# Two-layer hybrid block on one Trainium2 core: the second block's attention rewritten around pairs of query blocks

## The chip, the cores and the metric

One NeuronCore of a Trainium2 chip runs the whole kernel in one launch. The metric is the device time of one execution in microseconds (us). The engines named below are TensorE (PE; its weight loads are listed as PEld), VectorE (DVE), ScalarE (ACT), GpSimd (POOL) and SyncE (SP), which here issues every DMA.

## What is computed

The program is a first block (a state-space layer, two small attentions and gates) followed by a second block of two layers. The change is inside the second block. There a layer l of the reference does, for 512 latent rows `x` and 256 context rows `xc` of width 2048:

```python
q, k, v, up, uf, g = split_proj(h @ w_in[l])          # 8 query heads, 2 key/value heads of 128
q = apply_axial_rope(rmsnorm_2(q, q_norm_g[l]), cos, sin); k = ...
att = latent_attention(q, k, v, kc, vc)               # softmax over 256 context + 512 latent keys
out = merge_branches(att, up, uf, g, ...)             # concat(att, pool, fourier) * silu(g) @ w_out
x_new = x + gate[:, None] * out
if not last:                                          # layer 0 only
    attc = context_attention(qc, kc, vc)              # context queries, context keys only
    xc = xc + gate_c * merge_branches(attc, upc, ufc, gc, ...)
```

Everything is float32. Large products are made on PE as three products of split operands: each operand is a high part (rounded to the type fp32r) and a low part, the rest, and the sum is hi·hi + hi·lo + lo·hi. Products of plain float32 operands are issued as such, and the trace shows each of them as two matmul records.

## The kernel before

The stages run one after the other, each in a block of its own (`nc.Block()`), with a barrier between blocks. For each of the two layers of the second block: `projections(l)` makes 36 tiles of 128 columns of `h @ w_in` into the DRAM tensor `proj2` (tiles 0 to 7 queries, 8 and 9 keys, 10 and 11 values, 12 to 19 pool and Fourier input, 20 to 27 their gates, 28 to 35 the gates of the eight heads), and beside the tiles does the norms, rotations and the two mixing branches, which go to `mixd`. Then `attention(...)` computes the eight heads, and `out_projection` multiplies by `w_out`.

In `attention` the work is cut into units. A unit is one head and 128 queries. In layer 0 (768 columns: 512 latent, 256 context) a head has six units: four latent ones with 768 keys and two context ones with 256 keys, the context ones first and last. In layer 1 (512 columns) a head has four latent units. Per unit g:

- PE `scores(g)`: plain float32 products of queries and keys (L1417) into one of two PSUM buffers;
- DVE `peak(g)`: maximum over the keys (L1508), times -scale (L1510);
- ACT `exp(g)` with the sum over the keys (L1476, and a short read of the accumulator);
- DVE: reciprocal of the sum (L1525); POOL: a diagonal 128x128 matrix with the reciprocals (L1462);
- PE: six (or two) 128x128 transposes of the probabilities (L1434) into PSUM, and DVE copies them out (L1529) into `pt`.

After the last unit of a head, PE multiplies a matrix of ones by the diagonals (L1442), which gives 1/sum for every query, and makes values times probabilities for the whole head in plain float32 (L1446 for the 512 latent columns, L1449 for the 256 context columns of layer 0). ACT makes the tanh of the gate (L1491), DVE finishes silu (L1535), multiplies by 1/sum (L1539) and by the result (L1548), ACT and DVE split the result into high and low part (L1499, L1514) for the output projection. The head's slice of `mixd` is split too (L1494, L1542). Order on each engine is as written; engines wait for each other's counters. On SP the load of the next head's queries (L1378) stands behind the gate load (L1390), the `mixd` load (L1393) and, in the first head, behind four loads of 1 MB of `w_out` (L409, `prime`).

Of the kernel before, what the change touches and what calls it, by code (L numbers as in the profile page):

```python
# [11 lines left out]
F32 = mybir.dt.float32  # L12
F32R = mybir.dt.float32r
I32 = mybir.dt.int32
ALU = mybir.AluOpType
# [3 lines left out]
P = 128  # L19
# [97 lines left out]
def program(nc, cp, const, rope2, cn_sn, cs, invcnt, pos, x_in, mem_in, ctx_in, w_in, w_mem, w_glu,  # L117
            w_out, w_in2, w_out2, ada_w, ssm_b, ssm_c, pool_w, four_w, out):
    ctx = ExitStack()
    with ctx:  # L120
# [81 lines left out]
        odd_copied, shifted = count("odd_copied"), count("shifted")  # L202
        row_out = [count(f"row_out{i}") for i in range(4)]
# [1131 lines left out]
        def attention(heads, group, units, nkeys, qcols, q_src, k_src, v_src, g_src, chunk0, then, mixed=False):  # L1335
# [11 lines left out]

            th, res, g_sb = take(W if mixed else qcols)[:, 0:qcols], take(W if mixed else qcols)[:, 0:qcols], take(qcols)
            if mixed:
                q_sb, k_sb, v_t = ([xw[:, q * W:q * W + n]] for q, n in ((13, qcols), (14, nkeys), (15, nkeys)))  # L1350
                v_t = v_t[0]
            else:
                q_sb, k_sb, v_t = [take(qcols)], [take(nkeys)], take(nkeys)
# [6 lines left out]
            mix_sb = take(qcols) if mixed else None  # L1360
# [7 lines left out]
            with nc.Block() as block:  # L1368
                @block.sync
                def _(sp):  # L1370
                    for i in range(heads):
                        kv = i // group

                        if i > 1:
                            sp.wait_ge(s_ready.h, s_ready.at(nu * (i - 1)))

                        if i or not mixed:
                            sp.dma_start(q_sb[i % 2], q_src(i)).then_inc(loaded[i % 2].h, 16)  # L1378
                        if i % group == 0 and (i or not mixed):
# [5 lines left out]
                        if mixed and i == 1:  # L1385

                            for q in range(2):
                                sp.wait_ge(stored[q].h, stored[q].at(0))
                        sp.wait_ge(m2.h, m2.at(i))
                        sp.dma_start(g_sb, g_src(i)).then_inc(loaded[5].h, 16)  # L1390
                        if mixed:
                            sp.wait_ge(mixd_lo.h, mixd_lo.at(i))
                            sp.dma_start(mix_sb, mixd[i][:, 0:qcols]).then_inc(mixd_in.h, 16)  # L1393
                        if i == 0:
                            prime(sp, then)
# [69 lines left out]
                def _(act):  # L1465
# [15 lines left out]
                    for i in range(heads):  # L1481
                        for u_ in range(nu):
                            g = nu * i + u_
                            if g + 2 < total:
                                exp(g + 2)
                        act.wait_ge(loaded[5].h, loaded[5].at(16 * (i + 1)))
                        act.wait_ge(m5.h, m5.at(i))
                        if mixed and i == 0:
                            for q in range(2):
                                act.wait_ge(stored[q].h, stored[q].at(0))  # L1490
                        act.activation(th, g_sb, ACT.Tanh, scale=0.5).then_inc(m1.h, 1)  # L1491
                        if mixed:
                            act.wait_ge(mixd_in.h, mixd_in.at(16 * (i + 1)))
                            act.activation(h_hi[:, 8 + i, 0:qcols], mix_sb, ACT.Copy).then_inc(mixd_hi.h, 1)  # L1494
                        if (i + 1) % group == 0 and i + 1 < heads:
                            v_out(i // group + 1)

                        act.wait_ge(m5.h, m5.at(i + 1))
                        act.activation(h_hi[:, chunk0 + i, 0:qcols], res, ACT.Copy).then_inc(m6.h, 1)  # L1499

                @block.vector
                def _(dve):
# [16 lines left out]
                    for i in range(heads):  # L1519
# [20 lines left out]
                        if mixed:  # L1540
                            dve.wait_ge(mixd_hi.h, mixd_hi.at(i + 1))
                            dve.tensor_tensor(h_lo[:, 8 + i, 0:qcols], mix_sb, h_hi[:, 8 + i, 0:qcols].bitcast(F32),  # L1542
                                              ALU.subtract).then_inc(mixd_lo.h, 1)
# [19 lines left out]
            if mixed:  # L1563
                mixd_in.base += 16 * heads
                mixd_hi.base += heads
                mixd_lo.base += heads


# [387 lines left out]
        def projections(l):  # L1956
# [58 lines left out]
            p_gate = cnt  # L2015
            p_th = [sums[g % 2] for g in range(4)]
# [17 lines left out]
            with nc.Block() as block:  # L2034
# [127 lines left out]
                def _(act):  # L2162
                    st = Steps(act, va)

                    def read_out(n, par, segs_):
                        act.wait_ge(w_used.h, w_used.at(n + 1))

                        act.wait_ge(stored[par].h, stored[par].at(8 * (n - par)))
                        for a_, (a, b) in zip(accs(par, segs_), segs_):
                            ins = act.activation(stage[par][:, a:b], a_, ACT.Copy)  # L2170
                        ins.then_inc(staged.h, 1)
# [87 lines left out]
                def _(dve):  # L2259
# [36 lines left out]
                    if l:  # L2296
                        dve.wait_ge(rms_ready.h, rms_ready.at(2))
                        dve.reciprocal(inv_c, rms_c).then_inc(st.step(), 1)
                        dve.wait_ge(st.sem, st.now)
                    for iters, n0, segs, kind in parts:  # L2300
                        def body(i):
                            for j in range(4):
# [122 lines left out]
                        turns(st, iters, body, kind, 5 if kind == "qk" else 0)  # L2425
                    dve.wait_ge(st.sem, st.now)
# [175 lines left out]
            for s, v in ((rope_in, 32), (mix_in, 64), (sq_done, 12), (sums_done, 12), (root_done, 11), (qn_done, 11),  # L2602
                         (rot_done, 11), (rot_read, 10), (q_done, 10), (up_in, 64 * len(tok)), (uf_in, 64), (cnt_in, 64),
                         (pgate_in, 64), (fgate_in, 64), (pool_st, 64), (four_st, 64), (chan_done, 4), (odd_copied, 4), (y_copied, 4),
# [53 lines left out]
        for l in range(LAYERS):  # L2658
            last = l == LAYERS - 1
            projections(l)  # L2660
            units = [(b * P, 0, W) for b in range(TB)]
            if not last:

                units[0:0] = [(T, T, CT)]
                units[5:5] = [(T + P, T, CT)]
            width = T if last else W

            def gate(h):
                return row(proj2, h + 28)[:, 0:width]

            def query(h):
                return row(proj2, h)[:, 0:width]
            attention(HEADS2, HEADS2 // KV2, units, W, width, query, lambda kv: proj2[8 + kv], lambda kv: proj2[10 + kv],
                      gate, 0, lambda n: row(w_out2, n + 16 * l), mixed=True)
# [132 lines left out]
```

## Time and profile before

| what | value |
|---|---|
| runs | 3103.9, 3108.8, 3109.0 us (median 3108.8) |
| the profiled execution, its time | 3112.0 us |
| its span | 3110.3 us |
| PE busy | 2862.3 us (92%) |
| DVE, ACT, POOL busy | 51%, 31%, 14% |
| attention of layer 0, first score product to last result | 1839.5 to 2006.4 us |
| attention of layer 1, the same | 2765.5 to 2903.5 us |

A row of a timeline gives start, duration, engine, line, operation, output and inputs, count; in square brackets is how long the engine had been idle and whose end released it. PE's matmuls are pipelined, so the distance between the starts of neighbours is the cost of one, and a row's own duration is a little more. A row that groups instructions gives busy time, mean ns of one, and idle time before.

### The profile page before, as it was taken

The page shows a single profiled execution, that of the slowest core. Times are in us where ns is not written, and L with a number is a line of the kernel's source. Part 1 is how long each engine was busy: PE and PEld are TensorE (multiplying, and loading weights), DVE is VectorE, ACT ScalarE, POOL GpSimd, SP SyncE. Part 2 cuts the span into 40 slices and gives each one's busy share as a digit, 9 for nine tenths or more (in the row PEclk, how much of TensorE's full clock was granted, in tenths as well). Part 3 has the DMA queues.
Part 4 walks back from the last instruction along what each step waited for, and adds up shares of the span by engine and source line. Part 5 has one row for each costly group of instructions (what it writes and reads, how often), then busy time and mean ns, then how long its engine had stood idle before and what let it go on. Part 6 is the DMA issues. An engine that isn't in the chain of part 4 may idle for free. (4 is left out here: it accounts for less than half of the span.)

```text
span 3110.3 us, 35771 instructions
## 1 busy us (share of the span) xinstructions
PE 2862.3 (92%) x13746; PEld 2186.1 (70%) x13746; DVE 1596.3 (51%) x2138; ACT 956.8 (31%) x1601; POOL 450.5 (14%) x609
## 2 busy tenths in 40 slices
PE   7899999988448999999999998899989999989897
PEld 5666666676226867888888875488878877865685
DVE  6678778776554443125533337622243374547434
ACT  4444444443333333122211113311132232223221
POOL 2544444425101021000000001000010000001000
PEclk9999999999669999999999999999999999999998
DMA  5577777762123233233323332222213344431421
GB/s 196 189 303 291 289 299 285 302 241 100 48 88 108 95 126 125 75 115 132 115 100 133 120 136 69 102 76 93 89 77 118 138 163 145 164 135 62 156 95 54
DMA packets 111684, 447.15 MB, mean 144 GB/s; under 512 B 11440, under 2 KB 19760, under 8 KB 76208
## 3 DMA queue, kind: packets, MB, share of 16 engines
q1 hardware_dynamic: 111536, 445.16, 39.1%
q8 instruction: 95, 1.56, 0.2%
q14 instruction: 53, 0.43, 0.0%
HBM read 375.25 MB, written 69.86 MB: 143 GB/s over the span
## 5 line engine op out<-in xcount | busy, mean ns | idle before, releaser
L2524 PE MATMUL ps<-h_hi,w_hi 128*128 128x512 f32 x1600 | 576.9, 361 | 0.0
L2525 PE MATMUL ps<-h_lo,w_hi 128*128 128x512 f32 x1600 | 565.1, 353 | 0.0
L2526 PE MATMUL ps<-h_hi,w_lo 128*128 128x512 f32 x1600 | 561.4, 351 | 0.0
L384 PE MATMUL ps<-h_hi,w_hi 128*128 128x512 f32 (+1 forms) x1152 | 413.6, 359 | 37.7 <-DVE w_lo L343 37.7
L385 PE MATMUL ps<-h_lo,w_hi 128*128 128x512 f32 (+1 forms) x1152 | 412.6, 358 | 0.0
L386 PE MATMUL ps<-h_hi,w_lo 128*128 128x512 f32 (+1 forms) x1152 | 410.6, 356 | 0.0
L2524 PEld LDWEIGHTS ps<-h_hi,w_hi 128*128 128x128 f32 x1600 | 301.9, 189 | 49.8 <-issue 6.2
L2525 PEld LDWEIGHTS ps<-h_lo,w_hi 128*128 128x128 f32 x1600 | 301.7, 189 | 46.5 <-issue 6.2
L2526 PEld LDWEIGHTS ps<-h_hi,w_lo 128*128 128x128 f32 x1600 | 300.7, 188 | 43.6
L2305 DVE TENSOR_TENSOR w_lo<-raw,w_hi 128x2048 fp32r<-128x2048 f32 x64 | 146.4, 2288 | 310.6 <-ACT w_hi L2216 310.5
L2170 ACT ACTIVATE xw<-ps 128x512 f32<-128x512 f32 x112 | 53.9, 518 | 794.1 <-PE ps L2526 753.6
L384 PEld LDWEIGHTS ps<-h_hi,w_hi 128*128 128x128 f32 x1152 | 220.2, 191 | 73.3 <-DVE w_lo L343 41.2
L386 PEld LDWEIGHTS ps<-h_hi,w_lo 128*128 128x128 f32 x1152 | 219.4, 190 | 32.2
L385 PEld LDWEIGHTS ps<-h_lo,w_hi 128*128 128x128 f32 x1152 | 220.1, 191 | 30.8
L1462 POOL TENSOR_TENSOR wide<-ident_sb,stat 128x128 f32<-128x128 f32 x96 | 38.5, 401 | 1384.4 <-DVE stat L1525 1384.4
L1106 PE MATMUL ps<-h_hi,w_hi 128*128 128x512 f32 x512 | 203.2, 397 | 17.0 <-DVE w_lo L1015 9.5
L1108 PE MATMUL ps<-h_hi,w_lo 128*128 128x512 f32 x512 | 200.0, 391 | 0.0
L1107 PE MATMUL ps<-h_lo,w_hi 128*128 128x512 f32 x512 | 199.9, 390 | 0.0
L1900 ACT ACTIVATE wide<-xw 128x512 f32<-128x512 f32 (+3 forms) x48 | 33.8, 703 | 489.1 <-DVE stat L1924 379.2
L343 DVE TENSOR_TENSOR w_lo<-raw,w_hi 128x2048 fp32r<-128x2048 f32 x56 | 128.7, 2302 | 83.5 <-ACT w_hi L314 83.5
L1916 DVE SCALAR_TENSOR_TENSOR xw<-ps,mods,xw 128x512 f32 (+3 forms) x48 | 31.8, 662 | 260.0 <-PE ps L386 244.5
L1106 PEld LDWEIGHTS ps<-h_hi,w_hi 128*128 128x128 f32 x512 | 96.5, 188 | 60.3 <-DVE w_lo L1015 24.2
(370 smaller groups left out, 4672.8 us busy)
## 6 DMA issues: line engine op xcount, KB each, us to landing
raw<-w_in SPq DMA_DIRECT2D x112, 1024.0 KB, 5.1
raw<-ada_w SPq DMA_DIRECT2D x96, 1024.0 KB, 8.5
raw<-w_out SPq DMA_DIRECT2D x48, 1024.0 KB, 5.0
proj<-xw SPq DMA_DIRECT2D x60, 384.0 KB, 2.5
xw<-proj SPq DMA_DIRECT2D x70, 256.0 KB, 3.2
xw<-proj SPq DMA_DIRECT2D x46, 384.0 KB, 3.2
xw<-resid SPq DMA_DIRECT2D x8, 1536.0 KB, 12.7
proj<-wide SPq DMA_DIRECT2D x32, 256.0 KB, 11.1
```

What stands on the lines that cost most here:

```text
L343: dve.tensor_tensor(w_lo[:, j % 2, 0:size], raw[:, j, 0:size], w_hi[:, j % 2, 0:size].bitcast(F32), ALU.subtract).then_inc(lo_done.h, 1)
L384: pe.matmul(a_[q], wh, h_hi[:, h0 + k, lo:hi], start=k == 0, stop=False)
L385: pe.matmul(a_[q], wh, h_lo[:, h0 + k, lo:hi], start=False, stop=False)
L386: ins = pe.matmul(a_[q], wl, h_hi[:, h0 + k, lo:hi], start=False, stop=k == nk - 1)
L1106: pe.matmul(acc, wh, h_hi[:, k, 0:T], start=k == 0, stop=False)
L1107: pe.matmul(acc, wh, h_lo[:, k, 0:T], start=False, stop=False)
L1108: ins = pe.matmul(acc, wl, h_hi[:, k, 0:T], start=False, stop=k == KC - 1)
L2170: ins = act.activation(stage[par][:, a:b], a_, ACT.Copy)
L2305: dve.tensor_tensor(w_lo[:, j % 2, :], raw[:, j, :], w_hi[:, j % 2, :].bitcast(F32), ALU.subtract).then_inc(lo_done.h, 1)
L2524: pe.matmul(a_[q], wh, h_hi[:, k, a:b], start=k == 0, stop=False)
L2525: pe.matmul(a_[q], wh, h_lo[:, k, a:b], start=False, stop=False)
L2526: ins = pe.matmul(a_[q], wl, h_hi[:, k, a:b], start=False, stop=k == KC - 1)
```

## The change

`attention` loses its `mixed` branches and now serves only the first block. The second block's layers call the new `layer_attention`:

- Probabilities are scaled before they are transposed: POOL multiplies each unit's 128x768 (or 128x256) probabilities by the reciprocal of the sum, in place (a `tensor_scalar` with one operation). The diagonals and the product with ones are gone.
- The transposed probabilities are split: ACT copies PSUM to `pt_hi` (fp32r), DVE subtracts to `pt_lo`, in two pieces of 512 and 256 columns. The values are split too, once per key/value head.
- Values times probabilities are made for a pair of units (256 queries) as three fp32r products per 128 keys: 18 products of 256 columns for a latent pair, 6 for a context pair. Layer 0's units now stand latent, latent, context, context, latent, latent.
- The gates of the heads (tiles 28 to 35) are finished in `projections`: ACT reads those tiles out with tanh, where it copied before, and DVE adds one and multiplies by the tile (`gate_out`). In the attention one DVE operation per pair multiplies result, gate and 0.5; ACT and POOL split it.
- The low part of the `mixd` slice is made by POOL (before: DVE). Probabilities have three buffers (before: two), the values' load two, the gates two. The transposed unit has a single PSUM buffer, `t_a` and `t_b`, as before.

```diff
+                    def weighted(pr):
+                        i, q0, k0, nk = of(2 * pr + 1)
+                        pe.wait_ge(v_split.h, v_split.at(i // group + 1))
+                        pe.wait_ge(t_out.h, t_out.at(2 * pr + 2))
+                        pe.wait_ge(t_out_b.h, t_out_b.at(wide_ahead(2 * pr + 2)))
+                        pe.wait_ge(res_done.h, res_done.at(pr - 1))
+                        nch = nk // P
+                        for c in range(nch):
+                            vc = k0 // P + c
+                            x_hi, x_lo = pt_hi[pr % 2][:, c, :], pt_lo[pr % 2][:, c, :]
+                            pe.matmul(o_ps[pr % 2], v_hi[:, vc, :], x_hi, start=c == 0, stop=False)
+                            pe.matmul(o_ps[pr % 2], v_hi[:, vc, :], x_lo, start=False, stop=False)
+                            ins = pe.matmul(o_ps[pr % 2], v_lo[:, vc, :], x_hi, start=False, stop=c == nch - 1)
+                        ins.then_inc(o_ready.h, 1)
...
+                    for g in range(total):
+                        if g + 2 < total:
+                            scores(g + 2)
+                        turned(g)
+                        if g and g % 2 == 0:
+                            weighted(g // 2 - 1)
+                        if g == v_unit:
+                            pe.wait_ge(t_out.h, t_out.at(g + 1))
+                            pe.wait_ge(t_out_b.h, t_out_b.at(wide_ahead(g + 1)))
+                            values(1)
...
+                    for g in range(total):
+                        p_ = p_sb[g % 3][:, 0:of(g)[3]]
+                        pool.wait_ge(inverted.h, inverted.at(g + 1))
+                        pool.tensor_scalar(p_, p_, rs[g % ring], None, ALU.mult).then_inc(p_ready.h, 1)
+                        if g % 2 and g > 4:
+                            low((g - 5) // 2)
+                        if g % nu == 2:
+                            mixed(g // nu)
...
+                    for g in range(total):
+                        high(g)
+                        if g == v_unit:
+                            v_out(1)
+                        if g + 2 < total:
+                            exp(g + 2)
+                        if g % nu == 2:
+                            mixed(g // nu)
+                        if g % 2 and g > 2:
+                            result_high((g - 3) // 2)
...
+                    for g in range(total):
+                        if g + 2 < total:
+                            peak(g + 2)
+                        low(g)
+                        if g == v_unit:
+                            v_low(1)
+                        if g + 2 < total:
+                            invert(g + 2)
+                        if g % 2 and g > 2:
+                            result((g - 3) // 2)
...
+                            ins = act.activation(stage[par][:, a:b], a_, ACT.Tanh, scale=0.5) if gate else \
+                                act.activation(stage[par][:, a:b], a_, ACT.Copy)
+                        ins.then_inc(gate_tanh.h if gate else staged.h, 1)
...
+                    def gate_out(n):
+                        par, w_ = n % 2, parts[-1][2]
+                        dve.wait_ge(gate_tanh.h, gate_tanh.at(n - gates + 1))
+                        for q, (a_, (a, b)) in enumerate(zip(accs(par, w_), w_)):
+                            t_ = stage[par][:, a:b]
+                            ins = dve.scalar_tensor_tensor(t_, t_, 1.0, a_, ALU.add, ALU.mult)
+                            ins.then_inc(staged.h if q == len(w_) - 1 else st.step(), 1)
...
+                                if kind == "mix" and n > gates:
+                                    gate_out(n - 1)
...
+            layer_attention(l, lambda n: row(w_out2, n + 16 * l))
```

On POOL, in layer 1's attention, the last rows of the program before (L1462 is the diagonal, 32 of them in a row for 32 units):

```order
L2443 TENSOR_TENSOR h_lo<-xw,h_hi 128x512 x8
L2034 UNCONDITIONAL_BRANCH
L1454 UNCONDITIONAL_BRANCH
L1462 TENSOR_TENSOR wide<-ident_sb,stat 128x128 x32
L1368 UNCONDITIONAL_BRANCH
```

On POOL at the same place after the change, one head of layer 1 (L1684 scales a unit, L1673 makes the `mixd` slice's low part, L1679 that of a pair's result):

```order
L1684 TENSOR_SCALAR xw<-xw,stat 128x768 x2
L1679 TENSOR_TENSOR h_lo<-xw,h_hi 128x256
L1684 TENSOR_SCALAR xw<-xw,stat 128x768
L1673 TENSOR_TENSOR h_lo<-xw,h_hi 128x512
L1684 TENSOR_SCALAR xw<-xw,stat 128x768
L1679 TENSOR_TENSOR h_lo<-xw,h_hi 128x256
```

POOL went from one small operation per unit to one over all the unit's probabilities, plus three low parts per head.

On DVE, two units of layer 1 before (L1508 and L1510 peak, L1525 reciprocal, L1529 copy of the transposed unit):

```order
L1525 RECIPROCAL stat<-stat 128x1
L1529 COPY xw<-ps 128x6x128
L1508 TENSOR_REDUCE stat<-ps 128x1
L1510 TENSOR_SCALAR stat<-stat 128x1
L1525 RECIPROCAL stat<-stat 128x1
L1529 COPY xw<-ps 128x6x128
L1508 TENSOR_REDUCE stat<-ps 128x1
L1510 TENSOR_SCALAR stat<-stat 128x1
```

and two units after (L1753 and L1755 peak, L1774 and L1778 the low parts of the transposed unit, L1761 reciprocal, L1786 a pair's result):

```order
L1753 TENSOR_REDUCE stat<-ps 128x1
L1755 TENSOR_SCALAR stat<-stat 128x1
L1774 TENSOR_TENSOR w_lo<-ps,w_hi 128x4x128
L1778 TENSOR_TENSOR w_lo<-ps,w_hi 128x2x128
L1761 RECIPROCAL stat<-stat 128x1
L1786 SCALAR_TENSOR_TENSOR xw<-ps,xw 128x256
L1753 TENSOR_REDUCE stat<-ps 128x1
L1755 TENSOR_SCALAR stat<-stat 128x1
L1774 TENSOR_TENSOR w_lo<-ps,w_hi 128x4x128
L1778 TENSOR_TENSOR w_lo<-ps,w_hi 128x2x128
L1761 RECIPROCAL stat<-stat 128x1
```

The copy out became two subtractions behind ACT's copies, the reciprocal went behind them, and the head's long operations became one short one per pair.

On PE, the end of a head of layer 1 before (L1442 the product with ones, L1446 values times probabilities):

```order
L1434 MATMUL ps<-ident_sb,xw 128x128 x6
L1417 MATMUL ps<-wide 128x512
L1417 MATMUL ps<-wide 128x256
L1442 MATMUL ps<-wide,ones_sb 128x512
L1446 MATMUL ps<-xw 128x512 x6
L1434 MATMUL ps<-ident_sb,xw 128x128 x6
```

and two units of layer 1 after (L1612 scores, L1630 and L1635 transposes, then the first of the 18 products L1649 to L1651 of the pair before):

```order
L1612 MATMUL ps<-wide 128x512
L1612 MATMUL ps<-wide 128x256
L1630 MATMUL ps<-ident_sb,xw 128x128 x4
L1635 MATMUL ps<-ident_sb,xw 128x128 x2
L1612 MATMUL ps<-wide 128x512
L1612 MATMUL ps<-wide 128x256
L1630 MATMUL ps<-ident_sb,xw 128x128 x4
L1635 MATMUL ps<-ident_sb,xw 128x128 x2
L1649 MATMUL ps<-w_hi 128x256
L1650 MATMUL ps<-w_lo,w_hi 128x256
L1651 MATMUL ps<-w_hi,w_lo 128x256
```

The products that stood together at a head's end now follow every second unit, one pair late.

## Rows read from the trace of the kernel before

**Rows 1.** Page, part 1: busy us (share of the span) xinstructions.
```profile
PE 2862.3 (92%) x13746; PEld 2186.1 (70%) x13746; DVE 1596.3 (51%) x2138; ACT 956.8 (31%) x1601; POOL 450.5 (14%) x609
```

**Rows 2.** Stretches: length, busy of PE, PEld, DVE, ACT, POOL, PEclk, DMA, GB/s.
```profile
1839.00:2004.00 165.00, 144.19 (x556) 83.22 (x556) 117.05 (x231) 59.79 (x121) 19.23 (x48) 0.98 0.25 88
2764.00:2902.00 138.00, 121.81 (x444) 66.17 (x444) 91.19 (x167) 46.25 (x90) 12.82 (x32) 0.96 0.24 82
```

**Rows 3.** Timeline of SP: gate loads of neighbouring heads, layer 0, layer 1.
```profile
1960.42 0.34 SPq L1390 DMA_DIRECT2D xw<-proj  x1
1979.64 0.34 SPq L1390 DMA_DIRECT2D xw<-proj  x1
...
2867.42 0.34 SPq L1390 DMA_DIRECT2D xw<-proj  x1
2882.32 0.34 SPq L1390 DMA_DIRECT2D xw<-proj  x1
```

**Rows 4.** Timeline: last operation of each attention, layer 0, layer 1.
```profile
2005.47 0.96 DVE L1514 TENSOR_TENSOR h_lo<-xw,h_hi 128x768 fp32r<-128x768 f32 x1 [0.91 <-ACT h_hi L1499]
...
2902.79 0.69 DVE L1514 TENSOR_TENSOR h_lo<-xw,h_hi 128x512 fp32r<-128x512 f32 x1 [0.69 <-ACT h_hi L1499]
```

**Rows 5.** Timeline of layer 0: a head's products, then one latent unit.
```profile
1859.48 5.31 PE L1446 MATMUL ps<-xw 128*128 128x512 f32 x12
...
1868.39 0.90 ACT L1476 ACTIVATE xw<-ps,stat 128x768 f32<-128x768 f32 x1 [0.78 <-DVE stat L1510]
...
1869.44 0.96 DVE L1508 TENSOR_REDUCE stat<-ps 128x1 f32<-128x768 f32 x1
1869.44 0.87 PE L1434 MATMUL ps<-ident_sb,xw 128*128 128x128 f32 x6
...
1870.14 1.46 PE L1417 MATMUL ps<-xw,wide 128*128 128x512 f32 x4
```

**Rows 6.** Timeline of PE, layer 0's projections: fp32r products of 256 columns.
```profile
1145.67 0.28 PE L2454 MATMUL ps<-h_hi,w_hi 128*128 128x256 f32 x1
...
1146.03 0.28 PE L2454 MATMUL ps<-h_hi,w_hi 128*128 128x256 f32 x1
```

**Rows 7.** POOL: timeline with DVE beside it, then groups by form.
```profile
727.59 0.62 POOL L1232 TENSOR_SCALAR wide<-wide 128x512 f32<-128x512 f32 x1
728.29 3.08 POOL L1235 TENSOR_SCALAR wide<-wide 128x512 f32<-128x512 f32 x2
...
742.65 5.14 POOL L1235 TENSOR_SCALAR wide<-wide 128x512 f32<-128x512 f32 x2
...
742.19 2.52 DVE L1285 TENSOR_TENSOR w_lo<-raw,w_hi 128x2048 fp32r<-128x2048 f32 x1 [0.80 <-ACT w_hi L1255]
...
L2443 POOL TENSOR_TENSOR h_lo<-xw,h_hi 128x512 fp32r<-128x512 f32 x16 | 20.7, 1293 | 27.2 <-ACT h_hi L2193 27.2
...
L1462 POOL TENSOR_TENSOR wide<-ident_sb,stat 128x128 f32<-128x128 f32 x96 | 38.5, 401 | 1384.4 <-DVE stat L1525 1384.4
...
L565 POOL TENSOR_TENSOR h_lo<-xw,h_hi 128x256 fp32r<-128x256 f32 x16 | 11.2, 742 | 6.6 <-ACT h_hi L547 6.6
```

**Rows 8.** Groups by form: copies and a product that read PSUM, ACT and DVE.
```profile
L2170 ACT ACTIVATE xw<-ps 128x512 f32<-128x512 f32 x72 | 42.9, 596 | 794.1 <-PE ps L2526 753.6 <-PE ps L2509 40.5
L2170 ACT ACTIVATE xw<-ps 128x256 f32<-128x256 f32 x40 | 15.1, 378 | 0.0
...
L1539 DVE TENSOR_TENSOR xw<-xw,ps 128x512 f32<-128x512 f32 x12 | 8.2, 687 | 3.7 <-PE ps L1442 3.4
```

**Rows 9.** Timeline of PE: first scores of the second head, layer 0, layer 1.
```profile
1856.12 0.70 PE L1417 MATMUL ps<-xw,wide 128*128 128x256 f32 x2 [1.18 <-DMA wide<-proj]
...
2782.02 2.93 PE L1417 MATMUL ps<-xw,wide 128*128 128x512 f32 x4 [5.45 <-DMA wide<-proj]
```

**Rows 10.** Timeline of DVE, layer 1's projections: `w_lo` of tiles 34 and 35.
```profile
2735.83 2.28 DVE L2305 TENSOR_TENSOR w_lo<-raw,w_hi 128x2048 fp32r<-128x2048 f32 x1
...
2744.11 2.28 DVE L2305 TENSOR_TENSOR w_lo<-raw,w_hi 128x2048 fp32r<-128x2048 f32 x1
```

More of the change, by code:

```diff
@@ L202, in program @@
         odd_copied, shifted = count("odd_copied"), count("shifted")
+        t_ready_b, t_out_b, pt_hi_a, pt_hi_b, v_high, v_split, res_done, res_hi, res_lo, gate_tanh = (count(n) for n in (
+            "t_ready_b", "t_out_b", "pt_hi_a", "pt_hi_b", "v_high", "v_split", "res_done", "res_hi", "res_lo", "gate_tanh"))
         row_out = [count(f"row_out{i}") for i in range(4)]
@@ L1332, in glu, with attention @@
             four_st.base += 32
-        def attention(heads, group, units, nkeys, qcols, q_src, k_src, v_src, g_src, chunk0, then, mixed=False):
+        def attention(heads, group, units, nkeys, qcols, q_src, k_src, v_src, g_src, chunk0, then):
             nch = nkeys // P
@@ L1346, in take @@
                 return xw[:, at[0] - size:at[0]]
[L1348 to L1353, printed above, removed]
+            th, res, g_sb = take(qcols), take(qcols), take(qcols)
+            q_sb, k_sb, v_t = [take(qcols)], [take(nkeys)], take(nkeys)
             q_sb += [wide[:, 0:qcols]]
@@ L1359, in attention @@
             pt = take(nch * qcols).rearrange("p (c q) -> p c q", c=nch)
-            mix_sb = take(qcols) if mixed else None
             s_ps, t_ps, o_ps = [psum[0], psum[1]], psum[2], psum[3]
@@ L1375, in _ @@
                             sp.wait_ge(s_ready.h, s_ready.at(nu * (i - 1)))
-                        if i or not mixed:
-                            sp.dma_start(q_sb[i % 2], q_src(i)).then_inc(loaded[i % 2].h, 16)
-                        if i % group == 0 and (i or not mixed):
+                        sp.dma_start(q_sb[i % 2], q_src(i)).then_inc(loaded[i % 2].h, 16)
+                        if i % group == 0:
                             if kv > 1:
@@ L2015, in projections @@
             p_gate = cnt
+            gates = 28
             p_th = [sums[g % 2] for g in range(4)]
@@ L2168, in read_out @@
                         act.wait_ge(stored[par].h, stored[par].at(8 * (n - par)))
+                        gate = isinstance(n, int) and n >= gates
                         for a_, (a, b) in zip(accs(par, segs_), segs_):
-                            ins = act.activation(stage[par][:, a:b], a_, ACT.Copy)
-                        ins.then_inc(staged.h, 1)
+                            ins = act.activation(stage[par][:, a:b], a_, ACT.Tanh, scale=0.5) if gate else \
+                                act.activation(stage[par][:, a:b], a_, ACT.Copy)
+                        ins.then_inc(gate_tanh.h if gate else staged.h, 1)
                     act.wait_ge(raw_full[1].h, raw_full[1].at(16))
@@ L2425, in _ @@
                         turns(st, iters, body, kind, 5 if kind == "qk" else 0)
+                    gate_out(IN2 - 1)
                     dve.wait_ge(st.sem, st.now)
@@ L2660, in program @@
             projections(l)
[L2661 to L2674, printed above, removed]
+            layer_attention(l, lambda n: row(w_out2, n + 16 * l))
             out_projection(w_out2, 16 * l, [(0, T)] if last else both, l, then=None if last else lambda n: row(w_in2, n + IN2))
```

209 lines of the change are left out of this document (188 added, 21 removed).

## Prediction

> **What bounds the kernel now.** Read the page's busy table first: PE works 92% of the span [rows 1], nearly all of it in the projections, which the change leaves alone. So the stretches of the two attentions come next: 165 and 138 us, in which PE works 87 to 88%, DVE 71% and 66%, and POOL a tenth [rows 2]. A head costs 19.2 us in layer 0 and 14.9 us in layer 1, by the distance of neighbouring gate loads [rows 3]. The timeline of a unit shows why. A latent unit takes PE 0.70 us for six transposes and 2 x 0.43 + 2 x 0.215 = 1.29 us for scores (two records of 512 columns at 0.43, two of 256 at 0.215; 0.43 is the spacing of the 12 records that fill 5.31 us), 2.0 us in all; DVE takes about as much (0.96 maximum, a copy of the same size, two short ones) and ACT 1.1 [rows 5]. At a head's end PE alone works: 12 x 0.43 = 5.2 us of values, the product with ones 0.86, and in layer 0 another 4 x 0.215 and 0.43. That is 6.0 and 7.3 us per head in which DVE and ACT mostly idle. PE sets the pace, with a wait for probabilities here and there.
>
> **The change, part by part.**
>
> *PE.* Removed per head: 6.0 us (layer 1), 7.3 us (layer 0). Added: fp32r products of 256 columns at 0.12 us (three from one row to the next in 0.36) [rows 6], 18 per latent pair = 2.16 us, 6 per context pair = 0.72. A head's sum is 4 x 2.0 + 2 x 2.16 = 12.3 us in layer 1; in layer 0 4 x 2.0 + 2 x 0.65 + 2 x 2.16 + 0.72 = 14.3.
>
> *POOL.* It scales 768 columns per latent unit. The nearest rows are 512 columns wide, and they disagree by form. With one operation (L1235, as the new code has it) two take 3.08 us, spacing 1.54, while DVE is idle; with two operations (L1232) one takes 0.62 [rows 7]. Taking off the 0.2 us that the 256 and 512 wide subtractions (0.74 and 1.29) leave at width zero, 768 columns cost 1.3 x 1.5 + 0.2 = 2.15 us, 256 cost 0.85; by the two-operation row 0.8 and 0.4. I take 2.15, since the form is the same. With low parts of 0.74 per pair, the `mixd` slice 1.3 (512) or 1.8 (768), and 0.08 between operations, POOL needs 4 x 2.15 + 2 x 0.74 + 1.3 + 0.6 = 12.0 us per head in layer 1 and 4 x 2.15 + 2 x 0.85 + 3 x 0.74 + 1.8 + 0.9 = 15.2 in layer 0. POOL goes from idle to level with PE, a little above it in layer 0.
>
> The Trainium skill ("GPSIMD Engine Reference", Engine selection) says a one-input elementwise operation is "roughly line-rate" there; that would be some 0.65 us plus overhead for 768 columns, and the sum would be the first rival's. The row of 1.54 us for 512 columns speaks against it for this form, the row of 0.62 for it in the other.
>
> *ACT and DVE.* ACT per latent unit: exponential 0.99 (0.80 to its accumulator read, 0.19 for that), two copies 0.52 + 0.38 by [rows 8], half a result copy 0.2: 2.1 us. DVE: maximum and scaling 1.07, two subtractions about 0.62 + 0.35 (0.687 alone for 512 [rows 8]; a follower starts some 0.07 earlier), reciprocal 0.1, half a result 0.2: 2.35. Both lie under PE's 3.1 per unit. But they are chained. The transposed unit has one PSUM buffer, so from one unit's transposes to the next go 0.45 + 0.27 + 0.60 + 0.05 + 0.65 = 2.05 us (transposes, PE to ACT, copy, subtraction); where PE has less to do than that, as between layer 0's last unit of a head and the next head's first (1.1 us), it waits. DVE's reciprocal stands behind the exponential and in front of the next maximum; after an odd unit a result comes between (0.4), ACT waits for it, and the next unit's copies start about 0.9 late. Followed over two pairs in layer 1 this stretches a pair from 6.15 to 6.2 to 6.3 us, and once per head POOL's `mixd` slice adds 0.4. I take 12.7 us per head in layer 1. In layer 0 the buffer adds 1.1 us to PE's 14.3 and POOL asks for 15.2: I take 15.8.
>
> *Start of each attention.* The second head's queries still land behind the 4 MB of `w_out`: PE waits for them at 1856.1 and 2782.0 [rows 9]. The faster first head gains nothing; it waits longer. In front of the barrier `gate_out` of the last tile is now added, DVE about 0.7 us in layer 1 (512 columns, as L1539 in [rows 8]) and 1.2 in layer 0 (768), behind ACT's read-out, and all that follows shifts by it. The other seven tiles' `gate_out` stands on DVE behind `w_lo` of the tile to come: in layer 1 one `w_lo` ended at 2738.1 and the next began at 2744.1 [rows 10], and the mixing branch's work between them leaves DVE idle for half of it. So these cover each other, and I cost them at nothing; uncovered they would be 14 x 1 us.
>
> *Switch of the key/value head, once per layer.* Transposes, ACT's and DVE's splits of the values stand between two units: +2.8 us over a unit's pace; before it was some 2 us, inside the old heads.
>
> *End.* After the last transposes: copies and subtractions 2, last 18 products 2.2, result, copy and low part 1.7, 0.4 of latencies: 6.3 us. Before, they were followed by 5.2 or 6.0 us of values and long operations.
>
> **The sum.** Layer 1: queries at 2782.0 + 0.7; head 1's first unit passes scores, maximum, exponential, reciprocal and scaling in 5.9 (1.3 to 2 + 1.1 + 1.0 + 2.15); 27 units at 12.7/4 = 3.18 make 85.7; switch 2.8; end 6.3: 2883.4, against 2903.5 [rows 4]. That is -20. Layer 0: 1856.1 + 1.2, + 6.0, 41 units at 15.8/6 = 2.63 = 108.0, + 2.8, + 6.3: 1980.4, against 2006.4 [rows 4]: -26. In all -46. The profiled execution took 3112.0 us (span 3110.3), so 3066; the median of the runs is 3.2 lower, so 3063.
>
> **The rivals.**
>
> *POOL is cheap (3056).* If the scaling runs at the two-operation price, PE and the single buffer alone set the pace: 12.5 and 15.3 per head, and the first scaling is 1.3 us shorter in each layer. -1.4 - 1.3 - 3.4 - 1.3 on top: about -53. For it: the row of 0.62. Against: the rows of its own form.
>
> *POOL is somewhat dearer (3082).* At 2.6 us per 768 columns POOL's heads are 13.9 and 17.4, +8 and +11 us: about -27. The scaling takes its factor from memory, which no undisturbed row shows.
>
> *The chain serializes (3095).* Each of four engines waits for the next in every unit. If a head took 14 us in layer 1 and 18 in layer 0, the gain is 46 - 9 - 15 = 22, and with more lost at the switch and at the start some 15.
>
> *POOL is starved, slower than before.* Beside DVE's subtraction of two SBUF operands (2.52 us at 742.19) one of two scalings took 5.14 - 1.54 = 3.6 us instead of 1.54 [rows 7]: POOL got next to nothing meanwhile. At 2.3 times the price 768 columns would be 5 us, a head 23 us in layer 1 and some 29 in layer 0, and the kernel about 120 us slower (3230). It decides from 2.9 us per 768 columns: there POOL's head is as long as the old one. Against it: in the new loop DVE's long operations all read one operand from PSUM, and the 96 diagonals, made beside such operations, took 401 ns in the mean [rows 7]; even a quarter more is under the point.
>
> The skill's same page (Key points) names this: POOL contends with DVE instructions "with two SBUF inputs" or in a 2-port mode. By that rule this loop is free of it, since its DVE inputs come from PSUM and one SBUF tensor; the trace agrees in that the slow rows stand beside a two-SBUF subtraction.
>
> *The gain is not there (3109).* If the attentions were not on the path the time would stay; but nothing else runs in those stretches, and the output projection starts only behind the barrier.
>
> **How the numbers follow.** Forecast 0.50, cheap POOL 0.17, dearer POOL 0.15, serialized chain 0.09, starved POOL 0.06, no gain 0.03. The predicted time is the forecast's, 3063. Its lower bound is PE's own sum with no coupling: 27 x 0.1 + 41 x 0.25 less, 3050. The range takes in the first three cases with their spread: 3046 to 3090, leaving out the slow half of the serialized case and the two behind it. A measurement tells 0.2%, 6 us, from no change. Faster by more than that: 0.90. Same: 0.03. Slower: 0.07.
>
> **What would show it.** In the profile after: the scaling of 768 columns at 2.1 to 2.3 us (0.8: second case; 2.6: third; over 2.9: slower); neighbouring gate loads 12.7 and 15.8 us apart, in steady state; PE's wait for the second head's queries longer than 1.2 and 5.5 us and ending at the same times; the fp32r products 0.12 apart; PE's waits in front of its transposes released by POOL or by DVE's subtractions. If the low-part subtractions into the strided `pt_lo`, or ACT's copies into `pt_hi`, cost well over 0.69 and 0.60 for 512 columns, the chain sum is wrong. If the projections grow by more than 2 us, the gates were not hidden.

## The result: 25 us slower

| what | before | after |
|---|---|---|
| median of four runs each | 3106.4 us (3098.8 to 3109.0) | 3131.6 us (3129.0 to 3138.3) |
| ratio, 95% interval | | 1.0087, 1.0072 to 1.0102 |
| span of the profiled execution, granted clock | 3110.3 us, 0.961 | 3136.6 us, 0.950 |
| PE, POOL busy | 2862.3, 450.5 us [rows 1] | 2857.4, 628.2 us |
| attention of layer 0, first score to last result | 166.9 us | 175.9 us (from 1841.4) |
| attention of layer 1, the same | 138.0 us | 153.7 us (from 2776.3) |

The forecast was 3063. The two attentions grew by 9.0 and 15.7 us, together 24.7, of the 26.3 by which the span grew. So the loss is in the stretches where the gain was expected. The first look goes to the pace of the heads: SyncE's timeline of the changed kernel, the gate loads of neighbouring heads in layer 0, then in layer 1 (start, duration, queue, line, operation).

```profile
1964.49 0.34 SPq L1595 DMA_DIRECT2D xw<-proj  x1
1983.99 0.34 SPq L1595 DMA_DIRECT2D xw<-proj  x1
...
2837.03 0.34 SPq L1595 DMA_DIRECT2D xw<-proj  x1
2854.00 0.34 SPq L1595 DMA_DIRECT2D xw<-proj  x1
```

A head takes 19.5 us in layer 0 and 17.0 in layer 1, where the forecast had 15.8 and 12.7 and the old loop 19.2 and 14.9 [rows 3]. The windows of these two heads say who works in them (length; busy time of PE, PEld, DVE, ACT, POOL; granted clock; DMA share; GB/s).

```profile
1964.49:1983.99 19.50, 15.09 (x91) 11.27 (x90) 11.88 (x31) 10.50 (x27) 14.37 (x11) 1.00 0.18 61
2837.03:2854.00 16.97, 14.16 (x78) 10.61 (x77) 9.66 (x22) 8.30 (x19) 11.43 (x8) 0.90 0.14 48
```

No engine is full. POOL, which was to be level with PE, stands for 5 us of each head. The groups by form say for what: first the scaling, then the low part of the `mixd` slice (busy us, mean ns of one | idle time before them and its releaser).

```profile
L1684 POOL TENSOR_SCALAR xw<-xw,stat 128x768 f32<-128x768 f32 x64 | 140.7, 2204 | 1124.0 <-DVE stat L1761 1123.9
...
L1673 POOL TENSOR_TENSOR h_lo<-xw,h_hi 128x768 fp32r<-128x768 f32 x8 | 14.4, 1801 | 36.9 <-ACT h_hi L1730 36.9
L1673 POOL TENSOR_TENSOR h_lo<-xw,h_hi 128x512 fp32r<-128x512 f32 x8 | 10.1, 1263 | 41.4 <-ACT h_hi L1730 41.4
```

Of the 1124 us before the scaling, 650 and 459 lie before the first unit of each layer and cost nothing. The scaling itself is 2.20 us, forecast 2.15. What was not forecast is the last two rows: 78 us of idle time in front of 16 subtractions, about 5 us in each head, all for ScalarE's `h_hi` (line 1730). One head of layer 1 shows how that reaches PE. First POOL's timeline, then rows of ACT, DVE and PE from the same few us.

```profile
2842.44 2.21 POOL L1684 TENSOR_SCALAR xw<-xw,stat 128x768 f32<-128x768 f32 x1 [0.36 <-DVE stat L1761]
2849.83 1.26 POOL L1673 TENSOR_TENSOR h_lo<-xw,h_hi 128x512 fp32r<-128x512 f32 x1 [5.18 <-ACT h_hi L1730]
2851.07 2.20 POOL L1684 TENSOR_SCALAR xw<-xw,stat 128x768 f32<-128x768 f32 x1
```

```profile
2844.80 0.60 ACT L1716 ACTIVATE w_hi<-ps 128x512 fp32r<-128x512 f32 x1 [2.65 <-PE ps L1630]
...
2845.55 0.91 ACT L1700 ACTIVATE xw<-ps,stat 128x768 f32<-128x768 f32 x1
...
2847.48 0.60 ACT L1716 ACTIVATE w_hi<-ps 128x512 fp32r<-128x512 f32 x1
2847.97 0.38 ACT L1720 ACTIVATE w_hi<-ps 128x256 fp32r<-128x256 f32 x1
2848.24 0.91 ACT L1700 ACTIVATE xw<-ps,stat 128x768 f32<-128x768 f32 x1
2849.02 0.21 ACT L1700 ACTIVATION_READ_ACCUMULATOR xw<-ps,stat 128x1 f32 x1
2849.11 0.64 ACT L1730 ACTIVATE h_hi<-xw 128x512 fp32r<-128x512 f32 x1
...
2846.58 0.16 DVE L1761 RECIPROCAL stat<-stat 128x1 f32<-128x1 f32 x1
...
2849.06 1.46 PE L1612 MATMUL ps<-wide,xw 128*128 128x512 f32 x4
2853.33 0.66 PE L1630 MATMUL ps<-ident_sb,xw 128*128 128x128 f32 x4 [2.81 <-POOL xw L1684]
2854.04 2.29 PE L1612 MATMUL ps<-wide,xw 128*128 128x512 f32 x4
```

The loops are software-pipelined: in its pass g ACT first copies the transposed unit g, then makes the exponential of unit g + 2. POOL's pass g scales unit g, so POOL may be two units ahead of what ACT and PE are transposing. Both engines carry the `mixd` slice in their pass `g % nu == 2`. On POOL that place comes at 2844.6, after the scaling of the head's third unit. ACT gets to the same number only after it has copied that unit's transposes (2847.48 to 2848.35) and made the exponential of the fifth (2848.24): the slice's high part ends at 2849.75. Meanwhile the exponential of the fourth unit had long been made (it began at 2845.55) and its reciprocal was there at 2846.74, but its scaling stood behind the subtraction. So POOL gave up its lead, and then three things came in series that were meant to overlap: 1.26 of subtraction, 2.20 of scaling, and only then PE's transposes, after 2.81 us of waiting. After that wait the next four score products took 2.29 us instead of 1.46.

### The profile page after: what moved, and what is told of

Its sections match the earlier page's. It is cut to its first block and busy times, and to the rows that moved or that the text cites. A ratio compares the mean times of both kernels' runs of the same rounds, so it can differ in the third digit from the quotient of the medians.

```text
span 3136.6 us, 36731 instructions
## 1 busy us (share of the span) xinstructions
PE 2857.4 (91%) x14098; PEld 2229.1 (71%) x14098; DVE 1574.7 (50%) x2194; ACT 1004.3 (32%) x1757; POOL 628.2 (20%) x665
## 5 line engine op out<-in xcount | busy, mean ns | idle before, releaser
L1684 POOL TENSOR_SCALAR xw<-xw,stat 128x768 f32<-128x768 f32 (+1 forms) x80 | 155.4, 1947 | 1127.0 <-DVE stat L1761 1126.9
L2783 PEld LDWEIGHTS ps<-h_hi,w_hi 128*128 128x128 f32 x1600 | 301.9, 189 | 49.9 <-issue 6.2
L386 PEld LDWEIGHTS ps<-h_hi,w_hi 128*128 128x128 f32 x1152 | 220.0, 191 | 71.5 <-DVE w_lo L345 39.2
L2417 ACT ACTIVATE xw<-ps 128x512 f32<-128x512 f32 x88 | 42.1, 517 | 592.1 <-PE ps L2785 551.5
L1108 PE MATMUL ps<-h_hi,w_hi 128*128 128x512 f32 x512 | 204.2, 399 | 15.7 <-DVE w_lo L1017 8.2
L2159 DVE SCALAR_TENSOR_TENSOR xw<-ps,mods,xw 128x512 f32 (+3 forms) x48 | 31.8, 662 | 259.1 <-PE ps L388 243.2
L917 POOL TENSOR_TENSOR xw<-xw 128x32 f32<-128x32 f32 (+3 forms) x128 | 92.6, 723 | 254.3 <-ACT xw L973 254.3
```

Source lines behind the costliest of these rows:

```text
L386: pe.matmul(a_[q], wh, h_hi[:, h0 + k, lo:hi], start=k == 0, stop=False)
L1108: pe.matmul(acc, wh, h_hi[:, k, 0:T], start=k == 0, stop=False)
L1684: pool.tensor_scalar(p_, p_, rs[g % ring], None, ALU.mult).then_inc(p_ready.h, 1)
L2783: pe.matmul(a_[q], wh, h_hi[:, k, a:b], start=k == 0, stop=False)
```

## Experiments: was it this wait?

**Theory A**: a wait written at the same unit number on two engines that are two units apart costs POOL its lead once per head. Rivals: the scaling is simply too dear (B); TensorE is slowed by a lower granted clock in the attentions, whatever the order (C); or the gates' finish on DVE cost more than nothing (D). The kernels with ScalarE earlier, the cheaper scaling, both, and without gates were run beside one set of runs of the kernel before (3104.3 us), the other four beside a second set (3106.5); each ratio is to its own set. The changed kernel's own set had 3106.4, so 2 or 3 us between kernels of different sets say nothing, and small differences are read from the attentions of the traces.

**ScalarE earlier.** Nothing but ACT's pass for the slice is moved:

```diff
                     for g in range(total):
                         high(g)
 ...
-                        if g % nu == 2:
+                        if g % nu == 0:
                             mixed(g // nu)
```

> One part is moved: ScalarE makes the high part of the mixd slice in a head's first unit instead of its third; everything else is as in the changed kernel. Theory A (order): in the changed kernel GpSimd asks for that high part two units before ScalarE comes to it, so that once per head it loses its lead, idles 3.2 to 5.2 us, and TensorE waits for the next two scalings. Then this kernel has no idle of GpSimd before its mixd subtraction, heads of 13 us in layer 1 (16.9 now) and 16.2 in layer 0 (19.7 now), and some 50 us less: about 3078. Theory B (price): the 2.20 us scaling itself sets the pace; heads get under 1 us shorter: 3118 or more. Theory C (clock): TensorE is slowed by its granted clock of 0.85 to 0.9 in the attentions, whatever the order: clock and time stay within 5 us.

Measured: 3074.9 us (3068.7 to 3081.8), ratio 0.9914, 0.9881 to 0.9946: 57 us below the changed kernel's median by moving one line of ACT, with the same instructions. POOL's groups, then the windows of one head in layer 0 and one in layer 1:

```profile
L1684 POOL TENSOR_SCALAR xw<-xw,stat 128x768 f32<-128x768 f32 (+1 forms) x80 | 156.0, 1952 | 1150.3 <-DVE stat L1761 1150.2
L1673 POOL TENSOR_TENSOR h_lo<-xw,h_hi 128x768 fp32r<-128x768 f32 (+1 forms) x16 | 24.8, 1549 | 0.0
```

```profile
1933.72:1950.82 17.10, 15.05 (x92) 11.23 (x91) 11.67 (x31) 10.63 (x27) 14.50 (x10) 1.00 0.21 70
2779.88:2792.24 12.36, 12.36 (x77) 9.60 (x76) 9.36 (x22) 8.15 (x19) 11.39 (x8) 1.00 0.20 65
```

The wait is gone from all 16 subtractions, and PE works through the whole head of layer 1: 12.36 us of 12.36, against a sum of 12.3 in the forecast. A head of layer 1 got 4.6 us shorter, one of layer 0 2.4 (expected were heads of 13 and 16.2). The whole attentions, first the changed kernel's, then this one's:

```profile
1841.44:2017.29 175.85, 138.04 (x732) 101.91 (x732) 97.48 (x252) 86.52 (x212) 115.66 (x80) 0.90 0.22 82
2776.31:2929.98 153.67, 119.25 (x620) 88.72 (x620) 78.91 (x180) 68.11 (x156) 91.47 (x56) 0.87 0.21 74
...
1829.81:1983.38 153.57, 127.85 (x732) 95.23 (x732) 95.66 (x252) 87.51 (x212) 116.09 (x80) 0.96 0.26 94
2743.33:2862.31 118.98, 105.81 (x620) 80.75 (x620) 77.30 (x180) 67.25 (x156) 91.29 (x56) 0.96 0.27 95
```

They are 22.3 and 34.7 us shorter, 57.0 together. Not all of that is waiting: PE's busy time for the same products fell from 257.3 to 233.7 us, since the granted clock rose from 0.90 and 0.87 to 0.96. Rival C in its plain form falls, for the low clock did not stay "whatever the order"; how much the clock took is seen below.

**POOL later.** The same wait can be made harmless from the other side, with ACT left as it was:

```diff
-                        if g % nu == 2:
-                            mixed(g // nu)
+                        if g >= 4 and (g - 4) % nu == 0:
+                            mixed((g - 4) // nu)
+                    if nu == 4:
+                        mixed(total // nu - 1)
```

> Edit: as the changed kernel, ScalarE untouched (it still makes the high part of a head's mixd slice in its pass of the head's third unit), but POOL's subtraction for that slice stands two units later, behind the scaling of the head's fifth unit (layer 1: the next head's first). Theory A (POOL runs two units ahead of ScalarE, so a wait written at the same unit number costs it its lead once per head): POOL's mixd subtraction shows no wait, heads fall from 16.9 and 19.6 us to 12.4 and 17.1 as when ScalarE was made earlier, 3070 to 3080 us in all. Rival B (what helped in that run was ScalarE's order, its copy no longer lying between an exponential and the next copies): no gain here, 3120 to 3135 us.

Measured: 3077.2 us (3074.4 to 3087.2), ratio 0.9909, 0.9883 to 0.9936. POOL's subtraction waits for nothing again, and the attentions take 157.2 and 118.2 us:

```profile
L1673 POOL TENSOR_TENSOR h_lo<-xw,h_hi 128x768 fp32r<-128x768 f32 (+1 forms) x16 | 24.8, 1549 | 0.0
```

So it is not ACT's order that helped: what counts is the distance between the two places.

**Halfway.** ACT's slice in its pass `g % nu == 1`:

```diff
-                        if g % nu == 2:
+                        if g % nu == 1:
                             mixed(g // nu)
```

> Edit: as the changed kernel, but ScalarE makes the high part of the mixd slice in its pass of the head's second unit: halfway between the changed kernel (third) and the kernel that beat it (first). Theory A makes the price a matter of how far ahead POOL stands: one unit's lead is still asked for, so POOL waits some 0.5 to 2 us per head, and the time lies between the two, at 3080 to 3105 us. If the price were a switch (any disorder costs the same) it would be 3125 to 3135; if the second unit is early enough, 3070 to 3078.

Measured: 3084.3 us (3079.8 to 3087.7), ratio 0.9925, 0.9903 to 0.9947. POOL's group, and a head of layer 1:

```profile
L1673 POOL TENSOR_TENSOR h_lo<-xw,h_hi 128x768 fp32r<-128x768 f32 (+1 forms) x16 | 25.2, 1573 | 31.8 <-ACT h_hi L1730 31.8
...
2799.49:2813.05 13.56, 12.68 (x78) 9.54 (x77) 9.53 (x23) 8.26 (x19) 11.43 (x8) 1.00 0.18 60
```

The wait is 31.8 us in all, 2.0 per head, and a head of layer 1 13.6. By their ratios, 0.9925 and 0.9914, this kernel and the first are not apart; the traces separate them, with attentions of 156.2 and 127.2 us here against 153.6 and 119.0. The three places give 0, 32 and 78 us of waiting and 3075, 3084 and 3132 us: a price that grows with the lead that is given up, and faster than it. Part of the steeper end is the clock, which was 1.00 in this head and 0.90 in the changed kernel's.

**The wait without the work.** POOL still waits where it did, but subtracts 8 columns instead of 512 or 768 (the other columns' low parts are left out):

```diff
-                        pool.tensor_tensor(h_lo[:, 8 + i, 0:width], mix_sb[:, 0:width], h_hi[:, 8 + i, 0:width].bitcast(F32),
+                        pool.tensor_tensor(h_lo[:, 8 + i, 0:8], mix_sb[:, 0:8], h_hi[:, 8 + i, 0:8].bitcast(F32),
```

> Edit: as the changed kernel, with the wait for ScalarE's high part where it was, but POOL's subtraction for the mixd slice takes 8 columns in place of 512 or 768 (the low parts of the other columns are left out of the computation). That takes about 1.1 and 1.6 us of work per head off POOL and leaves the wait. If the wait alone is the cause: POOL still idles 3 to 5 us per head in front of it and the heads stay over 15 us in layer 1 and over 18 in layer 0, 3105 to 3120 us in all (each head shorter by about the work taken away, 8 x 1.1 + 8 x 1.6 = 21 us at most). If POOL's load is the cause and not the wait: the wait shrinks with it and the time falls to some 3080 us, near the kernel whose wait was taken away.

Measured: 3102.6 us (3093.7 to 3106.1), ratio 0.9982, 0.9970 to 0.9995, some 2 us under the range given for the wait. POOL's group and a head of each layer:

```profile
L1673 POOL TENSOR_TENSOR h_lo<-xw,h_hi 128x8 fp32r<-128x8 f32 x16 | 3.3, 205 | 77.4 <-ACT h_hi L1730 77.4
...
1930.27:1948.29 18.02, 15.18 (x92) 11.29 (x91) 11.90 (x32) 10.63 (x27) 12.91 (x11) 1.00 0.20 67
2810.18:2825.32 15.14, 12.67 (x78) 9.52 (x77) 9.58 (x22) 8.31 (x19) 10.34 (x8) 1.00 0.17 54
```

With next to no work left, POOL waits as long as before (77.4 against 78.2 us), and of the 57 us that the placement costs, 28 stay. These are the wait's alone: clock and PE's busy time are nearly those of the first kernel (0.96 in both attentions, 236.2 against 233.7 us). Where the wait has taken POOL's lead away, the work costs its whole length: in layer 0, where both heads shown were granted 1.00, the 1.5 us are the 1.6 of work removed. Where POOL has its lead, as in layer 1 of the first kernel, the same work costs nothing, since PE never stops there. In layer 1 a head got 1.8 us shorter by 1.06 of work. The granted clock was 1.00 here and 0.90 in the changed kernel's head, with 12.67 and 14.16 us of PE for the same products, so the clock has the remaining 0.8, and up to 1.5 if less of the work was on the path there; the runs don't separate the two.

**A cheaper scaling.** The same result by the form with two operations:

```diff
-                        pool.tensor_scalar(p_, p_, rs[g % ring], None, ALU.mult).then_inc(p_ready.h, 1)
+                        pool.tensor_scalar(p_, p_, rs[g % ring], 1.0, ALU.mult, ALU.mult).then_inc(p_ready.h, 1)
```

> One part is changed: the scaling on GpSimd is written with two operations (times the factor, times 1.0), whose row of before was 0.62 us for 512 columns; the order stays. Theory A: the scaling takes about 0.85 us for 768 columns instead of 2.20, GpSimd still idles before its mixd subtraction, and a head gains one to two of the differences that stand behind it: 1.4 to 2.7 us, so 3095 to 3112. Theory B: nearly the whole excess goes: heads of 13 and 16, about 3075. If the two-operation form with a factor from memory costs 2.2 us too, nothing changes.

Measured: 3090.3 us (3083.3 to 3099.2), ratio 0.9954, 0.9939 to 0.9970. The scaling of 768 columns and the subtractions after the edit, by form:

```profile
L1684 POOL TENSOR_SCALAR xw<-xw,stat 128x768 f32<-128x768 f32 x64 | 58.0, 907 | 1152.2 <-DVE stat L1761 1152.2
...
L1673 POOL TENSOR_TENSOR h_lo<-xw,h_hi 128x768 fp32r<-128x768 f32 x8 | 14.4, 1801 | 43.0 <-ACT h_hi L1730 43.0
L1673 POOL TENSOR_TENSOR h_lo<-xw,h_hi 128x512 fp32r<-128x512 f32 x8 | 10.1, 1262 | 48.2 <-ACT h_hi L1730 48.2
```

90 us of POOL's work go, 41 us of time, and its wait grows from 78 to 91 us. The time is 5 us under the range that theory A gave, and far from B's 3075. A layer 1 head falls from 17.0 to 14.1 us, but of these 2.9 us only 1.3, one scaling's difference, are less waiting of PE; 1.6 are PE's own busy time, 14.16 and 12.59, with the clock back at 1.00. In layer 0, at 1.00 before and after, the head falls from 19.5 to 17.4 us, more than one scaling and less than two. Rival B has a share then, but as part of the same chain, not as POOL's load: in the changed kernel's head of layer 1 POOL was busy 11.4 of 17.0 us.

**Both.** ACT earlier and the two-operation form:

> Both changes: ScalarE's mixd part in a head's first unit and the two-operation scaling. Theory A: GpSimd leaves the path, and TensorE with the single buffer sets it: heads of 12.5 and 15.3, about 3065; the second change brings about 10 us on top of the first. Theory B: the same as the scaling alone. Theory C: within 5 us of the changed kernel.

Measured: 3063.8 us (3061.1 to 3069.0), ratio 0.9874, 0.9843 to 0.9905. With the next one the fastest kernel of this study, 1.3% under the one before the change. Apart, the edits save 57 and 41 us, together 68: they cure the same chain. With the wait gone the cheap form is worth 11 us (11.4 by the attentions of the two traces, 272.6 and 261.2). A head of each layer:

```profile
1932.41:1948.63 16.22, 15.01 (x92) 11.24 (x91) 11.54 (x32) 10.62 (x27) 8.53 (x10) 1.00 0.22 74
2783.85:2796.23 12.38, 12.38 (x79) 9.61 (x78) 9.37 (x23) 8.16 (x20) 6.29 (x7) 1.00 0.20 64
```

Layer 1 gains nothing more by it, since PE fills the head already; layer 0 gains 0.9 per head and stays above the 15.3 that was expected.

**Both, and POOL later.** The edit of the second kernel on top of that:

> Edit: the fastest kernel so far (ScalarE's high part in the head's first unit, scaling in the form with two operations), with POOL's mixd subtraction two units later as well. With the cheap scaling POOL has a lead to spare, so neither place should show a wait; what is left over PE's sum is the one PSUM buffer of the transposes. Expected 3058 to 3066 us, equal to the 3064 of the kernel without this edit within 0.2%. Were the 1.3 and 1.8 us of the subtraction in front of the fourth unit's scaling still on the path, this would give back up to 0.5 us per head, 8 us.

Measured: 3064.4 us (3059.6 to 3068.9), ratio 0.9865, 0.9842 to 0.9889: no difference. Once there is a lead, it doesn't matter which of the two places the slice has.

**The gates.** The changed kernel with the gates of the heads left out of the projections, tanh and product both (the output lacks them):

```diff
-                        gate = isinstance(n, int) and n >= gates
+                        gate = False
 ...
-                                if kind == "mix" and n > gates:
-                                    gate_out(n - 1)
 ...
-                    gate_out(IN2 - 1)
```

> The finishing of the heads' gates in the projections is left out (ScalarE copies those tiles out as in the kernel before, VectorE does nothing on them), so the gates are missing from the output; the attentions are unchanged. If the gates are hidden, as the prediction had it, each attention starts 0.7 and 1.2 us earlier and the time falls by 2 us. If they are not, by up to 14 us.

Measured: 3129.3 us (3129.1 to 3130.2), ratio 1.0082, 1.0055 to 1.0108: 2 us under the changed kernel. That is the size of the forecast's 0.7 + 1.2, but no more than the runs of one kernel scatter. The traces say it more closely: from the end of layer 0's attention to the first scores of layer 1, a stretch that holds the second set of gates, go 759.1 us in the kernel before, 759.0 in the changed one and 759.3 without gates. Rival D falls: uncovered, the seven finishes of that layer would be some 7 us.

## Why the prediction was wrong

**The step that failed** is one half sentence in the paragraph on ACT and DVE: "once per head POOL's `mixd` slice adds 0.4". By the first experiment it measured 4.6 us per head in layer 1 and 2.4 in layer 0, and 57 us over both attentions, where 0.4 us in each of 16 heads would be 6. The forecast treated the slice as work that POOL has to fit in, 1.3 or 1.8 us in a budget. Followed as a wait, it would have asked when ACT gets to its own place for the slice. The two timelines of the loop were in the diff: POOL's place comes behind the scaling of unit 2, which needs the exponential that ACT makes in pass 0; ACT's comes in pass 2, behind the copies of unit 2 itself, whose transposes need that scaling. From that alone POOL must stand from the scaling of unit 2 through its transposes, both copies, an exponential and the slice's copy: 0.70 + 0.90 + 1.0 + 0.6 = 3.2 us by durations that the forecast had [rows 5, 8]. What is queued behind it is the next unit's scaling, and the subtraction of 1.3 stands before that too. The head shown had 5.2 us of the wait, since PE and ACT came to unit 2 later than its scaling was done (transposes at 2846.2, scaling done at 2844.65). So the rows of before give POOL's loss a lower bound, 4.5 us per head with the subtraction; what that costs a head they don't give. The forecast never asked any of it of this wait. What the runs showed in its place: 78 us of POOL waiting, with the subtraction, the scaling and PE's transposes in series behind it.

**The rest of the sum**, now that the wait can be taken out:

- POOL's scaling: 2.15 forecast, 2.20 measured (0.85 and 0.92 for 256 columns); without rounding 1.54 - 0.2 to 1.3 the forecast's own sum gives 2.21. The row of the same form was the right one to take, although the cheap form exists [rows 7].
- The products of 256 columns stand 0.12 us apart, as forecast [rows 6].
- Layer 1 without the wait: 119.0 us from first score to last result, 19.0 less than before, forecast 20 less. Head 12.36, forecast 12.7: PE's sum alone, 12.3, so the chain added nothing there.
- Layer 0 without it: 153.6 us, 13.3 less than before, where the forecast had 26. Its head is 17.1, not 15.8: seven periods make 9 of the 13 us. With the scaling at 0.9 us it is 16.2, of which PE works 15.0, not the 14.3 of the sum. So the 17.1 are PE's 15.0, 1.2 of waiting that the cheap scaling leaves (the forecast had 1.1 for the single buffer) and 0.9 that only the dear scaling brings, where the forecast added 0.4. The 0.7 on PE are in part no work: a row in front of a pause shows its whole length, 0.60 us for two score records of 0.215; how much of them, nobody counted. The other 4 us lie at the start and the end and were not followed.
- PE's wait for the second head's queries came in layer 1 (5.45 us, as long as before [rows 9] and not longer, as forecast; it ended 16.6 us after the layer's first scores, before 16.5). In layer 0 it did not come: the slower first head hid the load, and in the kernel with both edits 0.30 us of it are back.
- The gates: no cost that the stretch between the attentions shows, as forecast.

Here is PE's row for the second head's first scores in the changed kernel:

```profile
2792.95 2.93 PE L1612 MATMUL ps<-xw,wide 128*128 128x512 f32 x4 [5.45 <-DMA wide<-proj]
```

**The rivals.** The chain that serializes (14 and 18 us per head, 3095) was the nearest in kind: four engines wait for one another. It had no place and no mechanism, so its price was a guess, and its chance of 0.09 too. Starved POOL, the case meant for "slower", didn't occur: the scaling kept 2.20 us beside DVE's reads of PSUM throughout. The Trainium skill ("GPSIMD Engine Reference", Key points) names DVE instructions with two SBUF inputs or in a 2-port mode as those that contend with POOL; the trace agrees, in that 64 scalings beside DVE inputs from PSUM and one SBUF tensor took 2204 ns in the mean. The case that came, slower through a wait in the wrong place, was not among them.

**What the clock added.** Behind PE's wait of 2.81 us the scores at 2854.04 took 2.29 instead of 1.46 us and the next transposes 1.11 instead of 0.63 to 0.66, which is TensorE at the lower of its two levels for a part of them. The windows of the heads shown give the size: 14.16 us of PE at 0.90 in the changed kernel, 12.36 at 1.00 in the first experiment. So of the 4.6 us that a head of layer 1 lost, 2.8 are PE's wait and 1.8 slower products. In layer 0 the head shown kept 1.00, with PE at 15.1 of 19.5 us, but others did not: one from 1873.6 to 1895.3 was granted 0.84, with 18.0 us of PE.

Over both attentions the slower products are 257.3 - 233.7 = 23.6 of the 57 us, at most: with a faster PE some of it would have been waiting instead. The kernel with 8 columns shows less, 0.8 to 1.5 us per head of layer 1. The low clock came behind the waits and went with them, yet not with every wait: with 8 columns PE still waited about 2.4 us per head of layer 1, POOL as long as before, and each head shown was granted 1.00. What decides between the two is not shown. The wait costs 28 us without any of it.

## What to carry to other kernels

In a software-pipelined loop every engine has its own lead; before an operation with a wait is put in pass g of one engine, ask in which pass the engine that it waits for gets there, counted from what that pass itself depends on. An auxiliary step (a slice, a load, a split for later) belongs where its producer has been done for a pass, and the producer's part goes in as early as its input is there; moving one such line was worth 57 us here, more than the whole rest of the change. When a budget says that no engine is full and the time says otherwise, read the waits of the engine that runs ahead: 5 us of idleness once per head led to the cause here, on an engine that was busy two thirds of the time.

## What the runs showed of the hardware

GpSimd's multiplication by one factor per partition costs 2.204 us for 768 columns and 0.922 for 256 when written with one operation, and 0.907 and 0.48 when a second one, times 1.0, is added: 2.4 and 1.9 times as fast for more arithmetic, with the same result and no other difference in operands. The rows of 1.54 and 0.62 us for 512 columns in the kernel before [rows 7] had shown the same, with other surroundings as a possible reason; the edit leaves none. The Trainium skill ("GPSIMD Engine Reference", Engine selection) calls a one-input elementwise operation there roughly line-rate. The prediction made 0.65 us of that for 768 columns, 0.85 ns each. From 256 to 768 columns a column costs 0.84 ns in the form with two operations, so the trace agrees there; it costs 2.50 ns in the form with one, and there the trace disagrees.
